# Norm factors over 128x512: a product with ones, then root and reciprocal on the whole tile, at nine norms of a two-block model

## What is computed

```python
def rms_norm(x, w):
    y = xf * lax.rsqrt(jnp.mean(xf * xf, axis=-1, keepdims=True) + EPS)
    return (y * w.astype(jnp.float32)).astype(x.dtype)
...
    # in mamba2_mixer: a norm over each of 4 groups of 512 features
    yg = y.reshape(b, s, SSM_GROUPS, D_INNER // SSM_GROUPS)
    yg = yg * lax.rsqrt(jnp.mean(yg * yg, axis=-1, keepdims=True) + EPS)
    y = yg.reshape(b, s, D_INNER) * gnorm_w.astype(jnp.float32)
    return y.astype(h.dtype) @ out_w
```

## Time and profile before

| | us |
|---|---|
| median of three runs | 1428.01 |
| the three runs | 1424.14, 1428.01, 1429.1 |
| span of the profiled execution | 1425.8 |
| PE busy | 1385.0 |
| DVE busy | 837.1 |
| ACT busy | 661.1 |
| POOL busy | 533.9 |

### The profile page before, as it was taken

The page is one execution under the profiler, slowest core; times in us unless marked ns, Lnnn a source line. Parts: engine busy times, 40 slices in busy tenths (PEclk is TensorE's granted clock), DMA queues, the critical chain, the costliest instruction groups (busy, mean ns, idle before and its releaser), DMA issues.

```text
span 1425.8 us, 18177 instructions
## 1 busy us (share of the span) xinstructions
PE 1385.0 (97%) x6776; PEld 1093.3 (77%) x6776; DVE 837.1 (59%) x1441; ACT 661.1 (46%) x1126; POOL 533.9 (37%) x287
## 2 busy tenths in 40 slices
PE   8999999999999999989999999899999999999998
PEld 6877878777778878757888887675667888888887
DVE  6576464757557754785676412457756655554665
ACT  6654534635345543685555312245454332332553
POOL 2553553634320034456000433325353555545200
PEclk9999999999999999999999999989999999999999
DMA  5221223212223323111333333030002333232331
GB/s 186 89 74 60 89 60 89 75 59 74 74 79 93 96 87 91 59 60 31 91 101 107 88 141 93 31 104 30 16 16 89 95 98 98 94 103 90 117 91 60
DMA packets 33078, 116.82 MB, mean 82 GB/s; under 512 B 3932, under 2 KB 4316, under 8 KB 32736
## 3 DMA queue, kind: packets, MB, share of 16 engines
q1 hardware_dynamic: 31976, 111.85, 25.2%
q10 hardware_dynamic: 1016, 3.81, 0.8%
HBM read 113.55 MB, written 2.10 MB: 81 GB/s over the span
## 4 chain that ended last, share of the span: by engine, by line
PE 87%; DVE 5%; ACT 3%; issue 2%; POOL 2%; DMA 1%; ACTq 0%; DVEq 0%; POOLq 0%
PE bank L1279 84%; PE bank L1737 1%; PE bank L1580 1%; ACT wsh L854 1%; DMA h<-in_xT 1%; POOL wsl L698 1%; DVE arena L1895 0%; PE bank L1452 0%; POOL arena L756 0%; PE bank L1487 0%; ACT arena L1215 0%; DVE arena L2267 0%; ACT arena L936 0%; DVE arena L1975 0%; POOL arena L787 0%
## 5 line engine op out<-in xcount | busy, mean ns | idle before, releaser
L698 POOL TENSOR_TENSOR wsl<-ring,wsh 128x1024 fp32r<-128x1024 f32 x144 | 349.6, 2429 | 572.2 <-ACT wsh L854 572.1
L854 ACT ACTIVATE wsh<-ring 128x1024 fp32r<-128x1024 f32 x199 | 210.6, 1058 | 495.0 <-PE bank L1279 472.7
L1279 PE MATMUL bank<-parts1h,wsh 128*128 128x512 f32 (+1 forms) x736 | 293.3, 398 | 8.4 <-DVE parts1l L1818 2.3
L1279 PE MATMUL bank<-parts0h,wsh 128*128 128x512 f32 x704 | 283.3, 402 | 3.7 <-issue 1.3
L1279 PE MATMUL bank<-parts1l,wsh 128*128 128x512 f32 (+1 forms) x736 | 286.3, 389 | 0.0
L1279 PE MATMUL bank<-parts1h,wsl 128*128 128x512 f32 (+1 forms) x736 | 286.2, 389 | 0.0
L1279 PE MATMUL bank<-parts0l,wsh 128*128 128x512 f32 x704 | 275.3, 391 | 0.0
L1279 PE MATMUL bank<-parts0h,wsl 128*128 128x512 f32 x704 | 275.2, 391 | 0.0
L1279 PEld LDWEIGHTS bank<-parts1h,wsh 128*128 128x128 f32 x736 | 139.0, 189 | 44.4 <-issue 4.7
L1279 PE MATMUL bank<-arena 128*64 128x128 f32 (+9 forms) x964 | 153.3, 382 | 10.0 <-DVE arena L2320 3.7
L1279 PEld LDWEIGHTS bank<-parts0h,wsh 128*128 128x128 f32 x704 | 132.6, 188 | 38.5 <-issue 6.6
(11 more groups left out here) (313 smaller groups left out, 1835.2 us busy)
## 6 DMA issues: line engine op xcount, KB each, us to landing
ring<-in_wstream SPq DMA_DIRECT2D x206, 512.0 KB, 3.6
arena<-in_alibi ACTq DMA_DIRECT2D x2, 1024.0 KB, 5.0
outT<-arena SPq DMA_DIRECT2D x8, 256.0 KB, 2.6
h<-in_xT SPq DMA_DIRECT2D x2, 256.0 KB, 5.6
h<-in_xT ACTq DMA_DIRECT2D x2, 256.0 KB, 6.2
h<-in_xT SPq DMA_DIRECT2D x1, 512.0 KB, 8.5
h<-in_xT ACTq DMA_DIRECT2D x1, 512.0 KB, 9.1
arena<-in_cmpb ACTq DMA_DIRECT2D x1, 496.0 KB
```

Source lines behind the costliest of these rows:

```text
L698: return nc.gpsimd.tensor_tensor(dst, src, hi.bitcast(F32), ALU.subtract)
L854: nc.scalar.activation(wsh[n % NSET][:, :], src, ACT.Copy).then_inc(*done("high", ("high", L)))
L1279: return nc.tensor.matmul(*args, **kw)
```

## The change

Norms 0, 1, 3, 5 and 6 (`SPREAD`) and the four group norms are made otherwise; norms 2, 4 and 7 stay. DVE adds the eighth square too. At `norm` and `gn` PE makes one product of `ones` with `ssacc` or `yac`, 128x512, which holds the sum on all partitions. ACT takes the root of the 128x512 from the bank into `rt` or `ysq`. DVE takes the reciprocal of 128x512 into `rtb`, `rtb0` or `ysq`, at step `nb` for the norms and at `gn` for the groups. The column sums, the diagonal, the broadcast and the copy are gone, and with them the bank of `gb`. The tile products of norm `ssm` and of the groups read the factor from SBUF, not from a bank. In `gated` step `norm` stands one `pp` later. ACT's squares wait for the eighth addition where they waited for PE's sums.

```diff
+SPREAD = (0, 1, 3, 5, 6)
...
-        x = early(name, 5) + [("pp", i, m) for m in range(first, KD - 2)] + [("norm", ver)]
-        return x + [("pp", i, KD - 2), ("pp", i, KD - 1)] + early(name, 6) + early(name, 7) + [("nb", ver)]
+        x = early(name, 5) + [("pp", i, m) for m in range(first, KD - 1)] + [("norm", ver)]
+        return x + [("pp", i, KD - 1)] + early(name, 6) + early(name, 7) + [("nb", ver)]
...
-                        act.wait_ge(*at("mm", "ss", v))
+                        act.wait_ge(*(at("ssadd", v, q) if v in SPREAD else at("mm", "ss", v)))
...
+                if k == "norm" and a[0] in SPREAD:
+                    act.wait_ge(*at("mm", "ss", a[0]))
+                    nc.scalar.activation(rt[:, :], acc(("ss", a[0]))[:, :], ACT.Sqrt, bias=eps[:, 0:1], scale=1.0 / D)\
+                        .then_inc(*done("rms", ("rms", a[0]), ("accfree", "ss", a[0])))
...
-                    nc.scalar.activation(nrm[:, 2, :], ps(step)[:, 0:NT], ACT.Sqrt, bias=eps[:, 0:1], scale=1.0 / 512)\
+                    nc.scalar.activation(ysq, ps(step)[:, :], ACT.Sqrt, bias=eps[:, 0:1], scale=1.0 / 512)\
...
-                    if middle and kt == KD // 2:
-                        middle()
...
+                if k == "norm" and a[0] in SPREAD:
+                    pe.wait_ge(*at("ssadd", a[0], KD - 1))
+                    mm(b[:, :], ones, ssacc[:, :], start=True, stop=True).then_inc(*done("mm", ("mm", "ss", a[0])))
...
-                if k == "nb" and a[0]:
+                if k == "nb" and a[0] not in SPREAD:
                     broadcast(a[0])
...
-                    column_sums(b, 0, yac).then_inc(*done("mm", ("mm", *step)))
-                if k == "gb":
-                    b = open_bank(step)
-                    pe.wait_ge(*at("gdiag", a[0]))
-                    mm(b[:, :], ones, ysq, start=True, stop=True).then_inc(*done("mm", ("mm", *step)))
+                    mm(b[:, :], ones, yac, start=True, stop=True).then_inc(*done("mm", ("mm", *step)))
...
+                    if ver in SPREAD:
+                        ssadd(ver, KD - 1)
+                        continue
...
-                if k == "nb" and a[0] == 0:
-                    dve.wait_ge(*at("mm", "rb", 0))
-                    nc.vector.tensor_copy(rtb0, acc(("rb", 0))[:, :]).then_inc(*done("rtb", ("rtb", 0)))
+                if k == "nb" and a[0] in SPREAD:
+                    dve.wait_ge(*at("rms", a[0]))
+                    nc.vector.reciprocal(rtb if a[0] else rtb0, rt[:, :]).then_inc(*done("rtb", ("rtb", a[0])))
...
-                                                           acc(("rb", ver))[:, :],
+                                                           acc(("rb", ver))[:, :] if ver else rtb0,
...
-                    link(nc.vector.reciprocal(nrm[:, 3, :], nrm[:, 2, :]))
-                    nc.vector.tensor_tensor(ysq.rearrange("p (a b) -> p a b", a=NT), over(ident, NT, 1),
-                                            over(nrm[:, 3, :], P, 2), ALU.mult).then_inc(*done("gdiag", ("gdiag", g)))
+                    nc.vector.reciprocal(ysq, ysq).then_inc(*done("ginv", ("ginv", g)))
                 if k == "gb":
...
-                                                       ps(step)[:, :], ALU.mult, ALU.mult)\
-                            .then_inc(*done("ynf", ("ynf", g, m), *([("free", *step)] if m == GT - 1 else [])))
+                                                       ysq, ALU.mult, ALU.mult).then_inc(*done("ynf", ("ynf", g, m)))
```

More of the change, by code:

```diff
@@ L280, in jobs_of @@
         return []
-    if k in ("dtl", "dt", "cum", "upg", "upv", "proj", "pp", "out", "sout", "dn", "ao", "wo", "gate", "mq", "mk", "mo", "aq", "ak", "cmp_in", "gn", "gb", "mg"):
+    if k in ("dtl", "dt", "cum", "upg", "upv", "proj", "pp", "out", "sout", "dn", "ao", "wo", "gate", "mq", "mk", "mo", "aq", "ak", "cmp_in", "gn", "mg"):
         return [step, ("lg",)] if k == "cum" else [step]
@@ L343, in accs_of @@
     if k == "nb":
-        return [("rb", a[0])]
+        return [] if a[0] in SPREAD else [("rb", a[0])]
     if k == "nV" and a[1:] == (0, "c"):
@@ L904, in _ @@
                     link(nc.scalar.activation(tiny[:, :], eps[:, :], ACT.Sqrt))
-                if k == "norm" and a[0] < 7:
+                if k == "norm" and a[0] in SPREAD:
+                    act.wait_ge(*at("mm", "ss", a[0]))
+                    nc.scalar.activation(rt[:, :], acc(("ss", a[0]))[:, :], ACT.Sqrt, bias=eps[:, 0:1], scale=1.0 / D)\
+                        .then_inc(*done("rms", ("rms", a[0]), ("accfree", "ss", a[0])))
+                elif k == "norm" and a[0] < 7:
                     act.wait_ge(*at("mm", "ss", a[0]))
@@ L1293, in column_sums, with linear @@
                 return last
-            def linear(job, name, src, normed=None, middle=None):
+            def linear(job, name, src, normed=None):
                 b = open_bank(job)
@@ L1765, in _ @@
                 if k == "L" and a in RAW:
-                    linear(a, blocks_of(step)[0], xg, "raw" if a == RAW[0] else None, (lambda: broadcast(0)) if a == ("dtl",) else None)
+                    linear(a, blocks_of(step)[0], xg, "raw" if a == RAW[0] else None)
                 if k == "L" and a not in RAW:
@@ L1856, in _ @@
                             .then_inc(*done("hn_dve", ("hn", name, q)))
[L1857 to L1862 removed]
+                if k == "nb" and a[0] in SPREAD:
+                    dve.wait_ge(*at("rms", a[0]))
+                    nc.vector.reciprocal(rtb if a[0] else rtb0, rt[:, :]).then_inc(*done("rtb", ("rtb", a[0])))
+                if k == "nb" and a[0] == 4:
+                    dve.wait_ge(*at("mm", "rb", 4))
+                    nc.vector.tensor_copy(rtb1, acc(("rb", 4))[:, :]).then_inc(*done("rtb", ("rtb", 4), ("accfree", "rb", 4)))
                 if k == "hn":
                     ver = VERSION_OF[a[0]]
[L1865 removed]
+                    if ver:
+                        dve.wait_ge(*at("mm", "rb", ver))
+                    else:
+                        dve.wait_ge(*at("rtb", 0))
                     for name in a[:1]:
@@ L1877, in _ @@
                                                            vec[:, V_NORM[name] + m:V_NORM[name] + m + 1],
-                                                           acc(("rb", ver))[:, :],
+                                                           acc(("rb", ver))[:, :] if ver else rtb0,
                                                            ALU.mult, ALU.mult)\
                                 .then_inc(*done("hf", ("hf", name, m),
-                                                *([("accfree", "rb", ver)] if m == KD - 1 and name != "kv" else [])))
+                                                *([("accfree", "rb", ver)] if m == KD - 1 and name == "attn" else [])))
                             if m % 2:
```

2 lines of the change are left out of this document (1 added, 1 removed).

## The result

| | before | changed |
|---|---|---|
| median of 20 runs, us | 1428.95 | 1430.68 |
| lowest and highest | 1424.14, 1430.57 | 1427.14, 1433.68 |
| ratio to before, 95% interval | | 1.002 (1.0012 to 1.0029) |
| span of the profiled execution | 1425.8 | 1429.9 |

The change makes the kernel slower by 0.2%, 2 to 3 us (the medians lie 1.7 us apart, the ratio stands for 2.9), where 0.3% faster (1423.3 for 1428.0) was forecast. It is less than the 0.3% that were set as the line of no change, but its interval is clear of 1, and the time lies above the range that was given (1416.5 to 1428.5).

What follows compares the result with a forecast made beforehand. PE, busy 97% of the span, was taken to bound the kernel. Terms for norm ssm, four groups and four late norms summed to -4.75 us, taking the median from 1428.0 to 1423.3; range 1416.5 to 1428.5.

Steps and rivals of the forecast that it cites:

- The price of sums and broadcast: PE's queue at a norm: eight column sums cost 1.80 us, the broadcast product 0.87.
- the start of the tiles at norm `ssm`: First tile product at norm ssm starts at 28.55 instead of 27.84, +0.7 us, after the longer root and reciprocal.
- groups 0 and 1: First two group norms: a fill-in stretch covers the later factor, so they keep the saving, -0.9 and -0.95 us.
- the four late norms: Norms ple0, ple1, ln2 and ple2 keep most of PE's saving: -1.8, -1.4, -1.8 and -1.4 us.
- the 0.4 that `ple1` was to give back: At norm ple1, the longer root behind the table load and ACT's next weight block lose 0.4 us.
- rival (d): At nine places the 512-column product with ones costs 1.3 us each, giving back 3.9: 1427.2 us; chance 0.03.
- Group 2: +1.3: Third group norm: late factor users may meet POOL's weight subtraction; between -0.87 and +2.5 us, taken as +1.3.
- rival (b): DVE later at group 2 and norm ssm, reciprocal 4.4 us, clock falls at group 2: 1428.4, no change; chance 0.15.
- Norm `ssm`: +3.2: Norm ssm: later tiles 0.7, contention with POOL 1.5, clock 1.0 us; sum +3.2, between +0.7 and +6.3.
- Group 3: -1.0: Fourth group norm: the chain without the queued broadcast ends near 402.0 instead of 403.09; PE follows by 1.0 us.
- (c): SBUF-fed products and POOL's subtractions block one another at norm ssm and all four groups: 1432 us or more; chance 0.08.
- -4.75: Forecast sum in us over norm ssm, the four groups and the four late norms.

Runs made afterwards that it cites:

- `e4_norms_only`: Only norms ple0, ple1, ln2 and ple2 made the new way, norm ssm and the four groups as in the kernel before: 1421.8 us, ratio 0.9959.
- `twice_g0_g1`: Norm ssm and all groups with factors in PSUM banks, plus one extra thrown-away 128x512 reciprocal in groups 0 and 1: 1419.1 us, ratio 0.994.
- `bank_all`: The changed kernel, but norm ssm and all four groups write the reciprocal into a PSUM bank and tile products read it there: 1419.6 us, ratio 0.9947.
- `e2_gbank`: The changed kernel, but the four group norms' reciprocals write into the bank that held the sums; norm ssm's factor stays in SBUF: 1424.3 us, ratio 0.9977.

## Why the prediction was wrong

**What held.** The price of sums and broadcast (1.80 and 0.86 net), of the reciprocal (3.35 forecast, 3.35 measured), the start of the tiles at norm `ssm` (+0.7 forecast, +0.78 measured), groups 0 and 1, and the four late norms: -6.7 for them by the traces, -6.4 forecast (the 0.4 that `ple1` was to give back did not come), and 1421.8 for 1422 in `e4_norms_only`. The estimate of 4.3 us for the reciprocal, worked out from the Trainium skill ("VectorE: DVE Perf Modes", First, the fixed hardware budget), did not hold for this shape; the slope of the rows did. Nor did rival (d).

**The mechanism was in the text, and its size was wrong.** The step that failed is "Group 2: +1.3". It was put between -0.87 and +2.5, nearer to the second, and +2.5 was itself too low: the place took +5.37. (The lower end does not fit its own working, +0.8 less 0.9, which is -0.1; nothing hangs on it.) The upper end was right as far as it went: the third tile product ended at 340.64 in the times of before, for 340.65. But it stopped the chain there and took what follows as a fixed length. Measured from the moment behind PE's sums (-0.93), the rest is +6.30: 1.6 is the later start of the tiles against PE, which itself is early now; 1.8 the three tile products under the weight subtraction; 1.0 the fourth product under a subtraction of tiles; 2.0 the gates' split, and 0.25 the pass before it. Back come 1.1 at the low halves, which had been held by POOL before and are free now. That is 5.6 us at 351.63. The clock adds 2.1, and 1.4 is swallowed by the wait that stood at 349.74 before. Each late step shifts the next against POOL's own schedule, and on this path stood an instruction with a single source that POOL can hold up too. The prediction also looked for PE's wait at 349.74, where 1.34 us of waiting were to be had; it came earlier, at the product that had stood at 343.14 with no wait before it. The clock, which the text knew from the earlier trace rows, was counted once at norm `ssm` and left for rival (b) at group 2, though the wait there was put at some 3 us.

"Norm `ssm`: +3.2" came out at +4.80. The contention was put at 1.5 of at most 4.0 and took 1.8 (39.22 against 35.73, less 0.90 from the start and 0.78 of root and reciprocal). The clock took 2.2 for the 1.0 that was counted: PE's slack behind the place, a wait of 0.50, was too small to cover more.

"Group 3: -1.0" was right to the start of the tile products (1.0 earlier against the rest), but the fourth of them met POOL (1.77 us for 0.74) and PE waits 1.60 us for the low half made behind it: -0.16.

These three terms are 4.1 + 1.6 + 0.8 = 6.5 of the 8.9 us between -4.75 and the profiled execution's +4.1. The other 2.4 are mostly the start and the untouched stretch of the table (0.9 + 1.8), which lie in code that the change does not touch.

**The rivals.** The result lies between (b), 1428.4, and (c), 1432. Its mechanism is (c)'s, but at two places, not in all groups: groups 0 and 1 have the cover that the text named against (c), and `twice_g0_g1` shows that it would hold another 3.35 us. In the range, (c) had been left out as a case of 0.08. Pricing every collision of the rows in full (2.76 for 0.69), as (c) does, would have widened the range, but would not have given the result: with both hard places at their upper ends the sum is -4.75 + 3.1 + 1.2 = -0.45 us, still no slower than before. What was missing is the chain behind the third tile product. The Trainium skill ("GPSIMD Engine Reference", 1. Specifications) says that the SBUF interfaces are shared and names two-operand instructions; by it every collision had to count, and the rows of the two places show no exception: each tile product with both operands in SBUF that met a subtraction of POOL was held, or held it.

## What to carry to other kernels

When a factor moves from PSUM to SBUF, count who else reads SBUF: here the bank operand kept VectorE clear of GpSimd, and writing the long reciprocal's result back into the bank that held the sums turned a loss of 0.2% into a gain of 0.5% (`bank_all`), where 12.8 us, 0.9%, was the most that the change could give. Price a long instruction by the slack at each place, not by the engine's load: six of nine places took 3.35 us for nothing, two gave back more than all others won. And where a chain becomes late, follow it to PE's next product, for each step meets the other engines at a new time, and a wait of PE of 4 us cost another 1 to 2 in clock here.

## What the runs showed of the hardware

- A VectorE product with two SBUF operands waits for the end of a GpSimd instruction under way: up to 2.83 us for 0.69. It holds the other way round too: at norm `ssm` GpSimd's 2.79 for 2.38, begun under a tile product. With one operand in PSUM it runs at 0.74 beside it (the sixteen of `e2_gbank` take 0.743 on the mean).
- The reciprocal, with one operand, runs beside GpSimd unhindered: 3.30 us at 154.26 with a subtraction of 2.40 under it. That one writes into a bank; of those from SBUF to SBUF, the one at 25.29 in `e2_gbank` began 0.74 us before a subtraction of GpSimd ended (23.64 to 26.03) and took the same 3.35; none ran beside one for longer. But the gates' split, also with one, takes 2.47 to 2.53 for 0.48. The Trainium skill ("VectorE: DVE Perf Modes", What auto-detection actually checks) says that an instruction with a single source and its destination in SBUF runs in a mode that uses both ports, and the Trainium skill ("GPSIMD Engine Reference", 1. Specifications) counts such a mode among those in contention. The rows agree for the split, which does 512 columns in 0.48 us, less than the 0.69 of an addition; that the reciprocal has no such mode is what its freedom suggests, and no run here tests it by itself.
- Whether PE's clock falls behind a wait: it did after 4.01, 3.47 (`e2_gbank`), 5.44 and 4.30 us, and not after 1.65. At one place of the program it goes either way: behind a wait of 2.48 us at 86.46 it fell in the kernel before, behind the same wait in `bank_all` it stayed up:

```profile
86.69 0.63 PE L1462 MATMUL bank<-con,arena 128*128 128x128 f32 x4 [2.48 <-ACT arena L838]
...
88.00:90.00 2.00, 2.00 (x13) 1.65 (x11) 2.00 (x3) 1.75 (x4) 0.94 (x1) 1.00 0.44 129
```

So the length of a wait doesn't settle it alone, and 1 to 2 us of difference between two profiles can be this; what settles it was not tried.
